# A two-block transformer forward pass: key rotation in its own buffers by two queues, query tiles taken at once, attention steps in pairs

## The chip, the cores and the metric

The kernel runs on one core of one Trainium2 chip. The metric is the device time of one execution in microseconds (us), as the median of several runs. Engines: TensorE (PE, with its weight loads shown as PEld), VectorE (DVE), ScalarE (ACT), GpSimd (POOL) and SyncE (SP), which issues most transfers.

## What is computed

Two layers of different kind run one after the other on a sequence of 512 tokens of width 1024, all in float32. The first has four mixing branches (short convolution, stick-breaking attention, state-space mixer, block attention), a gated merge and a feed-forward part of width 2816. The second, where most of the change lies, is

```python
h = rmsnorm_2(x, norm_g[l])
proj = h @ w_in[l]
q, k, v, za, u, vs, zs, gm = jnp.split(proj, IN_SPLITS_2, axis=-1)
q = partial_rope(q.reshape(B, S, ATT_HEADS, HEAD_DIM), pos)     # 16 heads of 64
k = partial_rope(k.reshape(B, S, ATT_KV_HEADS, HEAD_DIM), pos)  # 2 heads, rotation on 16 of 64 rows
a = window_sink_attention(q, k, v, att_sinks[l])                # 64 queries see 192 keys at most
a = (a * jax.nn.silu(za)) @ w_att_out[l]
sgo = chunked_spatial_gating(gelu(u), gelu(vs), ...)
sgo = (sgo * jax.nn.silu(zs)) @ w_sg_out[l]
ga, gs = jnp.split(jax.nn.sigmoid(gm + b_merge[l]), 2, axis=-1)
x = x + (ga * a + gs * sgo) @ w_o[l]
```

## The kernel before, in words

**Weights in units.** All large products run over units of 256 weight columns (1 MB, eight tiles of 128 rows). SP loads a unit into one of two slots of `raw`; ScalarE rounds it to `whi` (line 1106, `split`); GpSimd subtracts to get the low part `wlo` (line 503, in halves of 128 columns, counted by the semaphore `lo_done`). TensorE then makes each output tile of 128 x 512 from 24 products: for eight rows of weights high by high and high by low (lines 569, 570), and after them eight low by high (line 577). Two units (n = 8 and 11) and the four `vs` units are token-major (`gemm_tm`, lines 591 to 593, 256 columns a product, the three kinds in turn). SP may load unit n once unit n-2 has its low part.

**Banks.** Tile T goes to one of four PSUM banks G[T % 4] and waits (`free_before`) until VectorE has taken tile T-4 (`tile_free`). In the stretch of the second layer's attention only two of them serve products, since the joined pair `gemm23` holds the scores of every odd step (`mix01` those of every even one): from the tiles of unit n_qz+2 on, tile T waits for tile T-2.

**Second layer, first part.** Unit n_e0 holds keys and values of both key heads; then come four pairs p of a query unit (n_qz+2p, two tiles) and a gate unit `za` (n_qz+2p+1, two tiles), then four units `vs` (n_vs to n_vs+3), then n_ga. Every 128 rows of queries hold two heads, and the rotation needs rows 0 to 7 and 8 to 15 of each head exchanged: VectorE writes the product times sine to `rope_s` (line 1988) and times cosine to `rope_q` (1989), SP exchanges rows from `rope_s` into `rope_t` with four transfers (`swap_rotary`, line 454, after both tiles are taken), and VectorE adds (line 1982). In the order of VectorE this sum stands before the first `za` tile of the same pair is taken (line 1511, reached from 1993). The keys use the same `rope_s` and `rope_t`, by eight transfers (line 466), and are summed at line 1905 after the first query product is ready.

**Attention in steps.** 32 steps (8 pairs of heads by 4 blocks of 128 queries) lie between the products. A step s is: scores on TensorE (`w_scores`, line 930, array in quarters of 64 x 64), maximum on VectorE (1919, 1920), exponential on ScalarE (1339, 1341), normalising on VectorE into `wp` (1926, 1927, 1932), transposing on TensorE (`w_turn`, 941), copying on ScalarE (1350, 1352), product with the values on TensorE (`w_values`, 953), and after every fourth step the result times the gate (1940, 1359, 1946). Each engine has a function `w_slot` with a counter `pos`, called at fixed places: on TensorE in each slot i the scores of step i, the values of step i-4, the transposition of step i-3. Slots lie after half of a tile's first part and after every even tile, at most six for each pair p from p = 1, then four in each `vs` unit and four in n_ga.

**The start.** TensorE runs seven idle products on a zero tile (line 645) until the first part of x, the identity and the parameters are in, transposes x tile by tile (`turn_in`, 637) and works on the first weight tile between the transpositions (661 to 663). The identity and the parameters come by ScalarE's queue, x and the weights by SP's.

Of the kernel before, what the change touches and what calls it, by code (L numbers as in the profile page):

```python
# [75 lines left out]
def build_program(nc, x, par, cst1, cst2a, w_in, w_branch, w_o, w_gu, w_down, w_in2, sg_w, sg_b, ln_g,  # L76
# [8 lines left out]
    with ctx:  # L85
# [99 lines left out]
        rope_s = place("rope_s", [P, 2, SEQ], Z0 + 40)  # L185
        za_e = place("za_e", [P, 2, SEQ], Z0 + 12)
# [77 lines left out]
        STEPS, W_PER = KD * TT, 6  # L264

        def w_bank(s):

            return (mix01, gemm23)[s % 2][:, :].rearrange("p (h c) -> p h c", h=2)[:, :, 0:192]

        def w_cols(s, i):  # L270

            return (mix01, gemm23)[s % 2][:, 448 + 4 * i:448 + 4 * i + 2]
# [76 lines left out]
        def _(sp):  # L349
# [12 lines left out]
            a_cols = (IN_XA, IN_BG, IN_CG, IN_X, IN_BC, IN_Z, IN_QD, IN_KD, IN_VD, IN_QB, IN_KB, IN_VB)  # L362
            load_x(0)
# [92 lines left out]
            for p in range(4):  # L456
                for j, c0 in enumerate((I2_Q, I2_ZA)):
# [90 lines left out]
        def _(pe):  # L548
            mm = nc.tensor.matmul

            def gemm_fm(T, n, s, xh, xl, kts, col, first, whi_=whi, wlo_=wlo, hook=None, ready=None):
# [11 lines left out]
                half = (3 * kts // 2 + 1) // 2  # L563
                for k in range(kts):
# [6 lines left out]
                    if hook and k == half - 1:  # L571
                        hook()
# [3 lines left out]
                for k in range(kts):  # L576
                    last = mm(bank[:, :], wlo_[:, s, k, col:col + P], xh[:, k, :], start=False, stop=(k == kts - 1))  # L577
                last.then_inc(sem("tile_done"), 1)

            def gemm_tm(T, n, c0, w_cols, per_bank, hook=None):  # L580
# [4 lines left out]
                pe.wait_ge(sem("lo_done"), 2 * n + 2)  # L585
                for i in range(per_bank):
                    t = i if per_bank == TT else (T % 2) * per_bank + i
                    o = bank[:, i * w_cols:(i + 1) * w_cols]
                    for k in range(KD):
# [9 lines left out]
            def unit_fm(n, xh=hh, xl=hl, kts=KD, after=None, hook=None, ready=None):  # L599
                for j in range(2):  # L600
                    gemm_fm(tiles_before(n) + j, n, n % 2, xh, xl, kts, j * P, j == 0, hook=hook,
# [38 lines left out]
            def first_tile():  # L640

                bank = G[0]
                pe.wait_ge(sem("warm"), 1)
# [54 lines left out]
            def st_cb(g):  # L698
                pe.wait_ge(sem("silu"), 4)
                if g == 0:  # L700
                    pe.wait_ge(sem("dtv_read"), 1)
# [161 lines left out]
            for f, (n0, part, h0) in enumerate(ffn_units):  # L863
                if f == 0:
# [3 lines left out]
                    unit_last_k(n0, hh, hl, KD, ("h2_lo", 0), sum_rows)  # L868
# [16 lines left out]
            unit_last_k(n_e0, hh, hl, KD, ("h3_lo", 0), sum_both, 1)  # L885
# [72 lines left out]
            def w_slot(limit):  # L958
                i = pos[0]
                if i >= limit and limit < STEPS:  # L960
                    return
                if i < STEPS:
                    w_scores(i)
                if 0 <= i - 4 < STEPS:
                    w_values(i - 4)
                if 0 <= i - 3 < STEPS:
                    w_turn(i - 3)
                pos[0] += 1

            for p in range(4):  # L970
                n = n_qz + 2 * p
                lim = W_PER * p
                for u in range(2):
                    for j in range(2):
                        gemm_fm(tiles_before(n + u) + j, n + u, (n + u) % 2, hh, hl, KD, j * P, j == 0,
                                hook=lambda: w_slot(lim))
                        if p == 0 and u == 0:
                            (turn_rows, turn_keys)[j]()
                        if j == 0:
                            w_slot(lim)  # L980
            for p in range(4):
                n = n_vs + p
                for j in range(2):
                    gemm_tm(tiles_before(n) + j, n, 0, UC, 2, hook=lambda: w_slot(STEPS))
# [10 lines left out]
            unit_fm(n_ga, hook=lambda: w_slot(STEPS), after=lambda j: w_slot(STEPS))  # L995
# [95 lines left out]
        def _(act):  # L1091
# [34 lines left out]
            act.dma_start(ident, cst1[:, 0:P]).then_inc(sem("start_in"), 16)  # L1126
            act.dma_start(prm[:, :], par).then_inc(sem("start_in"), 16)
            act.preload_act_table_set(EXP_LN)
            act.wait_ge(sem("start_in"), 32)
# [1035 lines left out]
```

## Time and profile before

| | us |
|---|---|
| Runs | 1363.51, 1366.31, 1366.41; median 1366.31 |
| Profiled execution | 1365.36 |
| its span, first to last instruction | 1363.3 |
| granted TensorE clock, mean over the span | 0.998 |
| TensorE busy | 1347.7 |
| VectorE busy | 615.5 |
| GpSimd busy | 596.7 |
| ScalarE busy | 513.6 |

The ends of matmuls are modelled: one of 128 x 512 is shown with 0.39 us, while the next one starts 0.23 us after it. So the distances between starts tell more of TensorE than its busy time.

### The profile page before, as it was taken

What the parts mean: (1) busy time and instruction counts of PE and PEld (TensorE: products, weight loads), DVE (VectorE), ACT (ScalarE), POOL (GpSimd) and SP (SyncE); (2) the same over time, 40 slices, a digit from 0 to 9 for tenths busy, and PEclk for the clock granted to TensorE, in tenths of its full rate; (3) what the DMA queues carried; (4) which work ended last, traced back from release to release, by engine and by line L of the source; (5) the groups of instructions that cost most, each with busy time, mean ns of one, the idle gap of its engine ahead of it and who ended that gap; (6) DMA issues with size and microseconds to landing.
All of it is one profiled execution on the core that took longest, in us unless ns stands there. A gap on an engine that the chain in (4) does not pass through costs nothing.

```text
span 1363.3 us, 17812 instructions
## 1 busy us (share of the span) xinstructions
PE 1347.7 (99%) x6852; PEld 1107.1 (81%) x6852; DVE 615.5 (45%) x1049; ACT 513.6 (38%) x751; POOL 596.7 (44%) x448
## 2 busy tenths in 40 slices
PE   8999999999999999999999999999999999999998
PEld 7878877788888888888888887777888888888887
DVE  3675434466544533213322347576765332242233
ACT  6222444555532443112221236244554323433233
POOL 4462333334444455444444546433322643525441
PEclk9999999999999999999999999999999999999999
DMA  6231241413223433233323223322221222222221
GB/s 203 80 107 62 78 135 51 147 39 95 72 97 101 147 93 92 93 101 102 105 93 93 85 70 108 101 66 70 94 63 62 94 91 93 93 93 94 92 93 62
DMA packets 146177, 126.43 MB, mean 93 GB/s; under 512 B 4352, under 2 KB 143744, under 8 KB 146112
## 3 DMA queue, kind: packets, MB, share of 16 engines
q1 hardware_dynamic: 145824, 125.40, 29.4%
q8 instruction: 46, 0.75, 0.2%
q10 hardware_dynamic: 288, 0.12, 0.0%
q14 instruction: 19, 0.16, 0.0%
HBM read 120.66 MB, written 2.10 MB: 90 GB/s over the span
## 4 chain that ended last, share of the span: by engine, by line
issue 41%; POOL 29%; PE 28%; ACT 1%; DVE 1%; DMA 0%; POOLq 0%; ACTq 0%; DVEq 0%
POOL wlo L503 28%; PE gemm L569 6%; PE gemm L570 6%; PE gemm L577 6%; PE gemm L591 1%; PE gemm L592 1%; PE gemm L593 1%; POOL wlo_b L499 1%; PE mix L953 1%; PE mix L941 1%; PE mix L1010 1%; PE gemm L619 0%; PE gemm L623 0%; PE gemm L620 0%; DVE sml L2022 0%
## 5 line engine op out<-in xcount | busy, mean ns | idle before, releaser
L503 POOL TENSOR_TENSOR wlo<-raw,whi 128x512 fp32r<-128x512 f32 x424 | 571.4, 1379 | 575.7 <-ACT whi L1106 575.7
L569 PE MATMUL gemm<-hh,whi 128*128 128x512 f32 x1128 | 445.9, 395 | 3.1 <-DVE za L1511 2.7
L570 PE MATMUL gemm<-hl,whi 128*128 128x512 f32 x1128 | 440.3, 390 | 0.0
L577 PE MATMUL gemm<-hh,wlo 128*128 128x512 f32 x1128 | 278.7, 389 | 0.0
L1106 ACT ACTIVATE whi<-raw 128x2048 fp32r<-128x2048 f32 x106 | 202.4, 1910 | 197.6 <-PE gemm L577 166.4
L569 PEld LDWEIGHTS gemm<-hh,whi 128*128 128x128 f32 x1128 | 212.4, 188 | 52.2 <-issue 4.7
L577 PEld LDWEIGHTS gemm<-hh,wlo 128*128 128x128 f32 x1128 | 211.8, 188 | 44.3
L570 PEld LDWEIGHTS gemm<-hl,whi 128*128 128x128 f32 x1128 | 212.5, 188 | 42.9 <-issue 0.2
L499 POOL TENSOR_TENSOR wlo_b<-raw_b,whi_b 128x512 fp32r<-128x512 f32 x16 | 20.7, 1291 | 152.2 <-ACT whi L1106 152.2
L1832 DVE TENSOR_TENSOR fu_t<-gemm,R 128x512 f32<-128x512 f32 x22 | 15.2, 692 | 99.7 <-PE gemm L577 99.7
L591 PE MATMUL gemm<-whi,hh 128*128 128x256 f32 x192 | 56.2, 293 | 0.4 <-POOL wlo L503 0.4
L592 PE MATMUL gemm<-whi,hl 128*128 128x256 f32 x192 | 54.3, 283 | 0.0
L593 PE MATMUL gemm<-wlo,hh 128*128 128x256 f32 x192 | 54.3, 283 | 0.0
L569 PE MATMUL gemm<-ah,whi 128*128 128x512 f32 x132 | 51.4, 390 | 0.5 <-DVE xT L1811 0.5
L570 PE MATMUL gemm<-al,whi 128*128 128x512 f32 x132 | 51.4, 389 | 0.0
L1123 ACT ACTIVATE gt<-gt 128x512 f32<-128x512 f32 x32 | 20.2, 631 | 75.2 <-DVE gt L1779 75.2
L1779 DVE TENSOR_TENSOR gt<-gemm,R 128x512 f32<-128x512 f32 x32 | 22.1, 689 | 57.7 <-PE gemm L577 57.2
L1302 ACT ACTIVATE fg_t<-fg_t 128x512 f32<-128x512 f32 x22 | 13.9, 632 | 84.6 <-DVE fg_t L1830 84.6
L1851 DVE TENSOR_TENSOR xT<-xT,gemm 128x512 f32 x16 | 11.0, 688 | 70.0 <-PE gemm L577 57.0
L591 PEld LDWEIGHTS gemm<-whi,hh 128*128 128x128 f32 x192 | 36.7, 191 | 1.3 <-issue 1.2
L592 PEld LDWEIGHTS gemm<-whi,hl 128*128 128x128 f32 x192 | 36.8, 191 | 0.2 <-issue 0.2
L1830 DVE TENSOR_TENSOR fg_t<-gemm,R 128x512 f32<-128x512 f32 x22 | 15.2, 692 | 48.1 <-PE gemm L577 39.8
(462 smaller groups left out, 1998.4 us busy)
## 6 DMA issues: line engine op xcount, KB each, us to landing
raw<-w_in SPq DMA_DIRECT2D x55, 1024.0 KB, 5.1
raw<-w_gu SPq DMA_DIRECT2D x44, 512.0 KB, 4.7
raw<-w_o SPq DMA_DIRECT2D x8, 1024.0 KB, 4.9
raw<-w_down SPq DMA_DIRECT2D x16, 512.0 KB, 4.0
raw_b<-w_branch SPq DMA_DIRECT2D x16, 256.0 KB, 5.3
raw<-w_ao SPq DMA_DIRECT2D x4, 1024.0 KB, 4.8
raw<-w_so SPq DMA_DIRECT2D x4, 1024.0 KB, 4.9
raw<-w_down SPq DMA_DIRECT2D x8, 384.0 KB, 3.7
```

What stands on the lines that cost most here:

```text
L499: nc.gpsimd.tensor_tensor(a(wlo_b), a(raw_b), as_f32(a(whi_b)), ALU.subtract)
L503: last = nc.gpsimd.tensor_tensor(a(wlo), a(raw), as_f32(a(whi)), ALU.subtract)
L569: mm(bank[:, :], w, xh[:, k, :], start=(k == 0), stop=False)
L570: mm(bank[:, :], w, xl[:, k, :], start=False, stop=False)
L577: last = mm(bank[:, :], wlo_[:, s, k, col:col + P], xh[:, k, :], start=False, stop=(k == kts - 1))
L591: mm(o, hh[:, k, tok], whi[:, s, k, w], start=(k == 0), stop=False)
L592: mm(o, hl[:, k, tok], whi[:, s, k, w], start=False, stop=False)
L593: last = mm(o, hh[:, k, tok], wlo[:, s, k, w], start=False, stop=(k == KD - 1))
L1106: fn(a(whi), a(raw), ACT.Copy).then_inc(sem("hi_done"), 1)
L1123: return fn(dst, src, ACT.Tanh, scale=scale)
L1779: tt(g, G[T % 4][:, :], R[:, :], ALU.mult).then_inc(sem("tile_free"), 1)
L1830: tt(fg_t[:, s, :], G[T % 4][:, :], R[:, :], ALU.mult).then_inc(sem("tile_free"), 1)
```

## The change

- The key rotation gets buffers of its own, `key_s` and `key_t`. Four of its transfers are issued by SP, four by ScalarE, as soon as `key_s` is written; queries no longer wait for the keys' `rope_t`.
- The joined pair of banks is now `gemm01`; products of the attention stretch use banks 2 and 3. Tiles of unit n_qz+2 wait for tile T-4, the restriction to T-2 holds from n_qz+3 to n_ga.
- VectorE takes query tiles directly after their products (`take_q`); in pair 0 the mixing weights, the keys and the constants come between, and the sum of the query pair (`finish_q`) after `za` tile 0 is taken. In the later pairs the order is written out, with slots between.
- An even slot has the scores of steps i and i+1, the values of i-4 and i-3 and the transposition of i-2, an odd slot the transposition of i-2 alone. Slots lie at fixed numbers of products in a tile (`W_AT`).
- Token-major units take all high products of a block first and wait for the low part of the weights after them.
- At the start the identity comes first on SP's queue, nine idle products run before it and eleven after the first two transpositions.
- Semaphores `dtv_read`, `h2_hi`, `h3_hi`, `h2_lo`, `h3_lo` are merged into others that count on.

```diff
@@ buffers and banks
+        key_s = place("key_s", [P, SEQ], Z0 + 80)
+        key_t = place("key_t", [P, 2, SEQ], Z0 + 28)
...
-        G = [ctx.enter_context(nc.psum_tensor(f"gemm{i}", [P, 512], f32)) for i in range(2)]
-        gemm23 = ctx.enter_context(nc.psum_tensor("gemm23", [P, 1024], f32))
-        G = G + [gemm23[:, 0:512], gemm23[:, 512:1024]]
+        gemm01 = ctx.enter_context(nc.psum_tensor("gemm01", [P, 1024], f32))
+        G = [gemm01[:, 0:512], gemm01[:, 512:1024]] + [ctx.enter_context(nc.psum_tensor(f"gemm{i}", [P, 512], f32)) for i in (2, 3)]
...
+        W_AT = ((12,), (4, 20), (12,), (4, 20))
+        W_END = STEPS + 5
...
-            return G[T % 2] if tiles_before(n_qz + 2) <= T < tiles_before(n_ga + 1) else G[T % 4]
+            return G[2 + T % 2] if tiles_before(n_qz + 2) <= T < tiles_before(n_ga + 1) else G[T % 4]
...
-            return T - 1 if tiles_before(n_qz + 2) <= T < tiles_before(n_ga + 2) else T - 3
+            return T - 1 if tiles_before(n_qz + 3) <= T < tiles_before(n_ga + 1) else T - 3
@@ sync
+            sp.dma_start(ident, cst1[:, 0:P]).then_inc(sem("ident_in"), 16)
             load_x(0)
...
                     if p == 0 and j == 1:
-                        sp.wait_ge(sem("tile_free"), tiles_before(n_e0) + 1)
-                        for r in (0, 64):
-                            for a, b in ((0, 8), (8, 0)):
-                                for kv in range(2):
-                                    sp.dma_start(rope_t[r + a:r + a + 8, kv, :], rope_s[64 * kv + b:64 * kv + b + 8, 0, :])\
-                                        .then_inc(sem("rope_in"), 16)
+                        sp.wait_ge(sem("key_s"), 1)
+                        for a, b in ((0, 8), (8, 0)):
+                            for kv in range(2):
+                                sp.dma_start(key_t[a:a + 8, kv, :], key_s[64 * kv + b:64 * kv + b + 8, :]).then_inc(sem("key_in"), 16)
                     if p >= 1 and j == 0:
-                        sp.wait_ge(sem("k_ready"), 1)
                         swap_rotary(p - 1)
@@ tensor, gemm_tm
-                pe.wait_ge(sem("lo_done"), 2 * n + 2)
                 for i in range(per_bank):
...
                     for k in range(KD):
-                        w, tok = slice(c0, c0 + w_cols), slice(t * P, (t + 1) * P)
                         mm(o, hh[:, k, tok], whi[:, s, k, w], start=(k == 0), stop=False)
                         mm(o, hl[:, k, tok], whi[:, s, k, w], start=False, stop=False)
+                    pe.wait_ge(sem("lo_done"), 2 * n + 2)
+                    for k in range(KD):
                         last = mm(o, hh[:, k, tok], wlo[:, s, k, w], start=False, stop=(k == KD - 1))
@@ tensor, first_tile
-                for i in range(7):
-                    mm(M[3][:, 0:P], warm, warm, start=True, stop=True)
-                pe.wait_ge(sem("start_in"), 32)
+                idle_products(9)
+                pe.wait_ge(sem("ident_in"), 16)
                 for m in range(2):
                     turn_in(m)
+                idle_products(11)
@@ tensor, w_slot
-                if i < STEPS:
-                    w_scores(i)
-                if 0 <= i - 4 < STEPS:
-                    w_values(i - 4)
-                if 0 <= i - 3 < STEPS:
-                    w_turn(i - 3)
+                if i % 2 == 0:
+                    for s in (i, i + 1):
+                        if s < STEPS:
+                            w_scores(s)
+                    for s in (i - 4, i - 3):
+                        if 0 <= s < STEPS:
+                            w_values(s)
+                if 0 <= i - 2 < STEPS:
+                    w_turn(i - 2)
@@ scalar
+            act.wait_ge(sem("key_s"), 1)
+            for a, b in ((0, 8), (8, 0)):
+                for kv in range(2):
+                    act.dma_start(key_t[64 + a:72 + a, kv, :], key_s[64 * kv + b:64 * kv + b + 8, :]).then_inc(sem("key_in"), 16)
@@ vector
+            v.memset(key_t[:, :, :], 0.0)
...
+                if i % 2 == 0:
+                    for s in (i, i + 1):
+                        if s < STEPS:
+                            w_soft(s)
+                if between:
+                    between()
+                if i % 2 == 0:
+                    for s in (i, i + 1):
+                        if s < STEPS:
+                            w_norm(s)
...
+                if p == 0:
+                    take_q(0)
+                    mixing_weights()
+                    take_q(1)
+                    finish_keys()
+                    attention_consts()
+                    take_za(0)
+                    finish_q()
+                    scale_x(0)
+                    take_za(1)
+                    scale_x(1)
+                    continue
+                w_slot()
+                take_q(0)
+                w_slot()
+                w_slot(lambda: take_q(1))
+                gate_attention(p - 1)
+                finish_q()
+                w_slot()
+                take_za(0)
+                w_slot(lambda: scale_x(0))
+                w_slot()
+                take_za(1)
+                scale_x(1)
```

## Rows read from the trace of the kernel before

**Rows 1.** Page, part 1: busy time, share of the span and instructions of each engine.
```profile
PE 1347.7 (99%) x6852; PEld 1107.1 (81%) x6852; DVE 615.5 (45%) x1049; ACT 513.6 (38%) x751; POOL 596.7 (44%) x448
```
**Rows 2.** TensorE's waits: line waited at and for, us in total, times, longest.
```profile
PE gemm L569 <- DVE za L1511: 2.7, 1, 2.7
...
PE gemm L591 <- POOL wlo L503: 0.4, 1, 0.4
```
**Rows 3.** Timeline, first query pair: start us, us, engine, line, operation, [idle before].
```profile
855.16 5.50 SPq L466 DMA_DIRECT2D rope_t<-rope_s  x8
...
866.85 2.64 SPq L454 DMA_DIRECT2D rope_t<-rope_s  x4
...
868.98 1.98 PE L577 MATMUL gemm<-hh,wlo 128*128 128x512 f32 x8
...
871.17 1.68 DVE L1982 TENSOR_TENSOR q<-rope_q,rope_t 128x1024 f32<-128x1024 f32 x1 [4.40 <-DMA rope_t<-rope_s]
...
873.63 0.80 PE L569 MATMUL gemm<-hh,whi 128*128 128x512 f32 x1 [2.68 <-DVE za L1511]
...
876.76 0.39 PE L570 MATMUL gemm<-hl,whi 128*128 128x512 f32 x1
```
**Rows 4.** Windows: stretch, us, busy of PE, PEld, DVE, ACT, POOL, clock, DMA, GB/s.
```profile
873.60:877.00 3.40, 3.37 (x9) 2.70 (x10) 2.27 (x3) 0.63 (x1) 0.38 (x1) 0.54 0.62 192
```
**Rows 5.** Timeline, one attention step between products of a query unit.
```profile
920.71 0.39 PE L569 MATMUL gemm<-hh,whi 128*128 128x512 f32 x1
920.94 0.39 PE L570 MATMUL gemm<-hl,whi 128*128 128x512 f32 x1
...
921.25 0.21 PEld L930 LDWEIGHTS gemm<-k,q 64*64 64x64 f32 x8 [0.35 <-issue]
...
921.74 0.42 PEld L953 LDWEIGHTS mix<-wpt,v 128*64 128x64 f32 x8 [0.28 <-issue]
...
921.95 0.57 DVE L1919 TENSOR_REDUCE gemm<-gemm 128x2 f32<-128x384 f32 x1 [0.81 <-PE gemm L930]
922.34 0.42 PEld L941 LDWEIGHTS mix<-c,wp 128*128 128x128 f32 x4 [0.17 <-issue]
...
922.75 0.47 PE L569 MATMUL gemm<-hh,whi 128*128 128x512 f32 x1
923.06 0.39 PE L570 MATMUL gemm<-hl,whi 128*128 128x512 f32 x1
```
**Rows 6.** Timeline, four transpositions between two tiles.
```profile
859.44 0.60 PE L904 MATMUL mix<-c,wpt 128*128 128x128 f32 x4
...
859.79 0.48 PE L569 MATMUL gemm<-hh,whi 128*128 128x512 f32 x1
```
**Rows 7.** Timeline, the start.
```profile
1.06 3.35 PE L645 MATMUL mix<-warm 128*128 128x128 f32 x14 [1.06 <-DVE warm L1524]
...
5.64 1.97 PE L637 MATMUL gemm<-c,xtm 128*128 128x128 f32 x8 [1.22 <-DMA prm<-par]
...
8.94 1.97 PE L637 MATMUL gemm<-c,xtm 128*128 128x128 f32 x8 [1.34 <-DMA xtm<-x]
...
19.59 0.39 PE L569 MATMUL gemm<-hh,whi 128*128 128x512 f32 x1
...
30.47 1.05 PE L830 MATMUL mix<-xbuf,c 128*128 128x128 f32 x8
```
**Rows 8.** Timelines of the vs units: TensorE's slots, one step's softmax.
```profile
973.45 0.56 PE L930 MATMUL gemm<-k,q 64*64 64x192 f32 x8
...
977.77 0.45 PE L930 MATMUL mix<-k,q 64*64 64x64 f32 x8
...
1009.93 0.16 DVE L1926 TENSOR_TENSOR mix<-mix,sml 128x2 f32<-128x2 f32 x1
1010.33 1.12 DVE L1932 TENSOR_TENSOR wp<-mix,sml 64x384 f32<-64x384 f32 x2
...
1010.52 0.41 ACT L1339 ACTIVATE gemm<-gemm,sml 128x192 f32<-128x192 f32 x1
```

More of the change, by code:

```diff
@@ L570, in gemm_fm @@
                     mm(bank[:, :], w, xl[:, k, :], start=False, stop=False)
-                    if hook and k == half - 1:
-                        hook()
+                    if hooks and 2 * k + 2 in hooks:
+                        hooks[2 * k + 2]()
                 if whi_ is whi:
@@ L577, in gemm_fm @@
                     last = mm(bank[:, :], wlo_[:, s, k, col:col + P], xh[:, k, :], start=False, stop=(k == kts - 1))
+                    if hooks and 2 * kts + k + 1 in hooks:
+                        hooks[2 * kts + k + 1]()
                 last.then_inc(sem("tile_done"), 1)
@@ L642, in first_tile, with idle_products @@
                 bank = G[0]
+                def idle_products(count):
+                    for i in range(count):
+                        mm(M[3][:, 0:P], warm, warm, start=True, stop=True)
                 pe.wait_ge(sem("warm"), 1)
-                for i in range(7):
-                    mm(M[3][:, 0:P], warm, warm, start=True, stop=True)
-                pe.wait_ge(sem("start_in"), 32)
+                idle_products(9)
+                pe.wait_ge(sem("ident_in"), 16)
                 for m in range(2):
                     turn_in(m)
+                idle_products(11)
                 for k in range(KD):
@@ L993, in pairs_after_first @@
                             gemm_fm((4 * p + T, T % 4), 2 * p + n0 + u, (n0 + u) % 2, h, l, KD, j * P, j == 0)
-            unit_fm(n_ga, hook=lambda: w_slot(STEPS), after=lambda j: w_slot(STEPS))
+            unit_fm(n_ga, hooks={4: w_slot})
             unit_last_k(n_ga + 1, ath, atl, KD, ("at_lo", 0))
@@ L1353, in w_turned, with w_out, w_slot @@
                 last.then_inc(sem("w_pt"), 1)
[L1355 to L1370 removed]
+            def w_out(m):
+                act.wait_ge(sem("w_o"), m + 1)
+                fn(ath[:, m, :], att_t[:, :], ACT.Copy).then_inc(sem("at_hi"), 1)
+            def w_slot():
+                i = pos[0]
+                if i % 2 == 0:
+                    for s in (i, i + 1):
+                        if s < STEPS:
+                            w_exp(s)
+                if 0 <= i - 2 < STEPS:
+                    w_turned(i - 2)
+                if i % TT == 3 and i >= 7:
+                    w_out((i - 7) // TT)
                 pos[0] += 1
@@ L1584, in st_dtT @@
                     last = tt(dtv[:, a], M[0][:, a], pcol("dtb", 0, 4), ALU.add)
-                last.then_inc(sem("dtv_read"), 1)
-                dve.wait_ge(sem("dtv_read"), 1)
+                last.then_inc(sem("dt_f"), 1)
+                dve.wait_ge(sem("dt_f"), 2)
                 link(ts(dts, dtv, -1.0, None, ALU.mult))
@@ L1878, in _ @@
             link(last)
-            stt(out=rope_s[:, 0, :], in0=G[T % 4][:, :], scalar=DH ** -0.5, in1=cs2[:, 1, :], op0=ALU.mult, op1=ALU.mult)
+            stt(out=key_s[:, :], in0=G[T % 4][:, :], scalar=DH ** -0.5, in1=cs2[:, 1, :], op0=ALU.mult, op1=ALU.mult)\
+                .then_inc(sem("key_s"), 1)
             for kv in range(2):
@@ new lines, in take_q, with finish_q @@
+                def take_q(j):
+                    T = tiles_before(n) + j
+                    tile_ready(T)
+                    tt(rope_s[:, j, :], bank_of(T)[:, :], cs2[:, 1, :], ALU.mult)
+                    tt(rope_q[:, j, :], bank_of(T)[:, :], cs2[:, 0, :], ALU.mult).then_inc(sem("tile_free"), 1)
+                def finish_q():
+                    dve.wait_ge(sem("rope_in"), 64 * (p + 1))
+                    b = 2 * p % 4
+                    tt(q2[:, b:b + 2, :], rope_q[:, :, :], rope_t[:, :, :], ALU.add).then_inc(sem("q_ready"), 1)
+                    dve.wait_ge(sem("q_ready"), p + 1)
@@ new lines, in take_za, with scale_x @@
+                def take_za(j):
+                    m, T = 2 * p + j, tiles_before(n + 1) + j
+                    tile_ready(T)
+                    if 4 <= m < 6:
+                        dve.wait_ge(sem("w_o"), m - 3)
+                    scaled(T, za_tile(m), 0.5)
+                def scale_x(j):
+                    m = 2 * p + j
+                    stt(out=xT[:, m, :], in0=xT[:, m, :], scalar=pcol("fg", m), in1=r1[:, :], op0=ALU.mult, op1=ALU.mult)\
+                        .then_inc(sem("x_scaled"), 1)
@@ L2013, in _ @@
                         gate_attention(3)
[L2014 to L2015 removed]
+                    w_slot()
+            while pos[0] < W_END:
+                w_slot()
             def layer_norm_stats():
```

165 lines of the change are left out of this document (55 added, 110 removed).

## The prediction

> **What bounds the kernel now.** I read the engines' totals first, then TensorE's waits, then the timeline around the longest wait, then the timeline of one attention step. TensorE is busy 99% of the span and the next engine 45% [rows 1], so only three things can shorten the run: time in which TensorE stands still, time at its low clock, and spacing between its instructions that the modelled ends hide. Of standing still the wait view has one large piece, 2.7 us until VectorE has taken a `za` tile, and one of 0.4 us for a low part of weights [rows 2].
>
> The timeline shows that piece [rows 3]. TensorE issues the last eight products of a tile from 868.98, and with 0.227 us from start to start (920.71 to 920.94 in [rows 5]) it would go on at 870.79. It goes on at 873.63: 2.84 us lost. The bank that tile n_qz+2 is to fill is freed only when VectorE takes `za` tile 0, and VectorE stands for 4.40 us before that at the sum that finishes the first query pair (line 1982), which waits for the four swap transfers issued from 866.85. The clock falls after this stop: the granted clock is 0.54 over 873.6 to 877 [rows 4], that is mostly its 1.2 GHz level, and the seven starts from 873.63 to 876.76 [rows 3] take 3.13 us where seven at 0.227 take 1.59: another 1.54 us. The place costs 4.4 us in all.
>
> The hidden spacing is in the 32 attention steps. One step [rows 5]: from the last product at 920.94 to the loads of the scores 0.31 us (0.23 between products); the scores' eight loads take 0.21, then 0.28 us of nothing before the values' loads; after those, 0.17 before the transposes; these go from 922.34 to 922.75; and the first product after them is followed by the next only after 0.31 us.
>
> **The change, part by part.**
> (a) *Query tiles taken at once, tile n_qz+2 in its own banks.* The swap of pair 0 is now finished after `za` tile 0 is taken, and tile n_qz+2 goes to banks 2 and 3, which wait for tiles four back instead of two. VectorE's new row in pair 0: query tile 0 at about 856, the mixing weights' copies (1.8 us), query tile 1 once TensorE has it near 859.5, keys and values to about 863, constants 1 us, `za` tile 0 at 865.5. The swaps go out from about 861, so have landed by 866 (2.6 us of issue and 1.7 until line 1982 starts, as in [rows 3]), and tile n_qz+2 asks only for query tile 1. The wait goes with its clock loss: minus 4.4. What is late next is pair 0's finished query, near 868, wanted by the first scores near 873.7: 6 us of slack.
> (b) *Key swaps by two queues.* Eight transfers now take SP 5.5 us [rows 3] and hold back the next weight load until 860.7 (855.16 and 5.50). Afterwards SP has four and ACT four, and they start when the keys' product is written (about 852.4) instead of at 855.2. SP's next load goes about 5 us earlier, which nothing needs at once: zero. ACT's four (0.7 us each by SP's row, 2.8 in all) and the wait stand in front of its split of unit n_qz+1, which then begins near 855 (852.4 and 2.8); it ends near 857, GpSimd's first half near 859.5, and TensorE asks for them at 859.8 and 863.3. Cover 2.8 us, cost zero; without it each us late is a us of stop. The two added memsets of VectorE (0.9 us) lie where it waits for ScalarE: zero.
> (c) *Steps in pairs.* A slot with an even number has two scores, two values, one transposition; an odd slot one transposition alone. Per pair one entry goes (0.31 less 0.23: 0.09) and one turn from scores to values and one from values to transposes, of which only the part that is not streaming is won: of the 0.28 us some 0.12 (192 columns in two passes are 0.16 at 2.4 GHz), of the 0.17 some 0.06. The lone transposition costs 0.35 (859.44 to 859.79, [rows 6]) instead of 0.41. Together 0.33 us. The end of the chain has one slot fewer. I take 0.34 for each of 16 pairs: minus 5.5. Bounds: 0 if the drains are all work, and 0.09 + 0.28 + 0.17 = 0.54, so 8.6 us, if none is.
> The Trainium skill ("TensorE: Matmul & The Clock Gate", section "Architectural detail: the array is 16× 32×32, not 1× 128×128") says that weight loads are pulled ahead of matmuls in flight; were that so between these forms, pairing would win nothing and the sum would be 5.5 us smaller. "TensorEngine Tiling (Array Packing)", section "Key Properties", of the same skill has it that a change of tiling mode drains the engine; the rows go with this one, since the loads do stand off.
> (d) *Order of the products in the token-major units.* Low parts of the weights are asked for after 16 products instead of before the first. The 0.4 us wait [rows 2] goes, with the restart about it: minus 0.6. In number and form the products are the same.
> (e) *The start.* The identity goes first on SP, 20 idle products instead of 7. Seven take 3.35 us from 1.06; the first transposes start at 5.64, the second at 8.94 when more of x has landed, and the first tile is over at 19.59 [rows 7]. With nine the engine works until 5.4, then on the first transposes, then on eleven more. At the low clock eleven take 11 × 0.48 = 5.3 us, from 7.5 to 12.8; at the high clock 11 × 0.26 = 2.9 (four products in 1.05, [rows 7]), from about 6.6 to 9.5. If they bring the high clock before the second transposes, those and the next eight products run at half their time, which the landing of x and the chain through ScalarE partly take back. I take minus 1.0. Bounds: plus 2, if the eleven run at the low clock and push everything, minus 2.5, if all that is slow between 8.94 and 13 is won.
> (f) Merged semaphores, the moved mixing weights and constants, the bank split itself: they move no work of TensorE. Zero; their cover is VectorE's free time.
>
> Sum: 4.4 + 5.5 + 0.6 + 1.0 = 11.5. The profiled execution took 1365.4 us (span 1363.3); the median of the runs, 1366.3, is 0.07% above it and inside the runs' own scatter. 1365.4 - 11.5 = 1353.9.
>
> **Rivals.**
> *Pairing wins nothing* (the drains are streaming). For it: the ends are modelled. Against it: entry and exit gaps are seen in starts. 1365.4 - 6.0 = 1359.4.
> *The stop comes back elsewhere in the first pair*: ScalarE's split behind key swaps, or tile n_qz+3, which now is the first to wait for a tile two back. Against it: slack of 2.8 us and more. Its price is the old one, 4.4: 1358.3.
> *The idle products cost*: 3 us against my term: 1356.9.
> *Slower: the next pair waits for the softmax of the last.* Before, a step's softmax had another step's time to spare; now the scores of a pair need both weights of the previous pair. Slots lie 4.32 us apart in the vs units (973.45 to 977.77, [rows 8]), so a pair has 8.3. Chain: scores to first reduction 0.7 us (921.25 to 921.95, [rows 5]), two of these 1.4, ScalarE 1.25 per step from 1010.52, then VectorE from line 1926 to the end of line 1932 1.5 per step (1009.93 to 1011.45): about 6.0. The slack is 2.3, and about as much where a query tile is taken between. It decides where the chain grows by 2.3 + 0.9: at 0.9 us per pair the 11.5 and a further 2.7 are gone. At 1.5 us per pair: 1353.9 + 24 = 1378.
>
> **How the numbers follow.** About 0.2% (2.7 us) is what a measurement of this kernel can tell from no change. Forecast 0.68; pairing wins nothing 0.11; stop elsewhere 0.09; idle products 0.05; softmax waits 0.07, of which 0.03 so mild that the sum lands within 0.2%. Faster 0.93, same 0.03, slower 0.04. I predict 1354.0. Range: down to 1349.5 (pairs at their upper bound, 3 us more, and 1.5 of scatter), up to 1361 (the first rival and 1.5).
>
> **What would show it.** The wait for line 1511 gone, the granted clock 1.0 from 871 to 884; the L591 wait gone; in an even slot two scores with one gap of loads behind, and in an odd slot transposes alone; from the first query unit to the end of the attention about 10 us less; the second transposes near 9 with high-clock spacing. It would be wrong if TensorE had waits at line 930 or 941 for VectorE's `wp`, or if an even slot took as long as two old ones.

## The result, and the profile after

The changed kernel takes 1353.92 us (median of four runs, 1353.55 to 1354.07) against 1366.05 us of the kernel before on the same chip (four runs, 1363.51 to 1366.41). The ratio is 0.9911, with an interval of 0.9899 to 0.9924. The forecast was 1354.0. The profiled execution took 1353.55 us, 11.8 less than the one before. The total is right; of its terms the start and the pairing are too small, one loss was missing, and these errors nearly cancel, as the rest shows.

Part 1 of the changed kernel's page, to be laid beside [rows 1]:

```profile
PE 1341.1 (99%) x6878; PEld 1110.9 (82%) x6878; DVE 619.2 (46%) x1050; ACT 513.2 (38%) x751; POOL 597.9 (44%) x448
```

TensorE remains the bound. Its 26 further instructions are thirteen more idle products at the start, two each, and yet it is busy for fewer us. Its waits, beside [rows 2] (line waited at and for, us in total, times, longest):

```profile
PE mix L649 <- DVE warm L1533: 1.1, 1, 1.1
PE gemm L623 <- issue: 0.9, 1, 0.9
...
PE gemm L570 <- ACT whi L1113: 0.4, 1, 0.4
...
PE mix L961 <- DVE att_t L1952: 0.4, 1, 0.4
```

The 2.7 us at a `za` tile and the 0.4 us for a low part are gone, and so are the two waits for x and the parameters at the start. One is new: the values' product waits 0.4 us for the gated output `att_t`. Waits of 0.2 us and less at transposes fall below the list.

Where the clock was at half speed [rows 4], it is now full for the whole first query pair. But another stretch has it at half, at 101.8 us. The windows of the changed kernel (columns as in [rows 4]):

```profile
98.40:101.80 3.40, 3.40 (x27) 3.18 (x26) 1.17 (x3) 0.00 (x0) 1.47 (x2) 1.00 0.23 42
101.80:105.20 3.40, 3.40 (x9) 2.62 (x9) 0.73 (x2) 0.00 (x0) 0.00 (x0) 0.50 0.76 267
...
870.00:884.00 14.00, 14.00 (x88) 10.79 (x87) 8.56 (x22) 5.92 (x21) 5.28 (x5) 1.00 0.24 76
```

The same stretch in the kernel before:

```profile
101.80:105.20 3.40, 3.40 (x22) 3.04 (x22) 1.21 (x4) 0.00 (x0) 0.37 (x1) 1.00 0.56 175
```

TensorE is busy throughout in both. With the granted clock at 0.50, its 1.2 GHz level, the products start 0.43 us apart instead of 0.23. The timeline of TensorE in the changed kernel shows what stands before the fall:

```profile
98.93 2.29 PE L702 MATMUL mix<-sml,c 128*128 128x4 f32 x20
101.08 0.49 PE L570 MATMUL gemm<-hh,whi 128*128 128x512 f32 x1
101.40 0.40 PE L571 MATMUL gemm<-hl,whi 128*128 128x512 f32 x1
...
101.93 0.63 PE L571 MATMUL gemm<-hl,whi 128*128 128x512 f32 x1
102.36 0.63 PE L570 MATMUL gemm<-hh,whi 128*128 128x512 f32 x1
102.78 0.63 PE L571 MATMUL gemm<-hl,whi 128*128 128x512 f32 x1
```

Twenty products of only four columns, the state mixer's cumulative sums, take 2.15 us from the first one's start to the next wide product; 0.7 us after that the clock falls. Laid beside the kernel before, product by product, the lead shrinks over these 3.4 us from 1.99 to 0.43: the fall costs 1.55 us. Nothing in the diff touches that place.

The start, beside [rows 7]:

```profile
1.06 4.21 PE L649 MATMUL mix<-warm 128*128 128x128 f32 x18 [1.06 <-DVE warm L1533]
5.06 1.60 PE L641 MATMUL gemm<-c,xtm 128*128 128x128 f32 x8
6.50 2.62 PE L649 MATMUL mix<-warm 128*128 128x128 f32 x22
8.96 1.04 PE L641 MATMUL gemm<-c,xtm 128*128 128x128 f32 x8
...
17.60 0.39 PE L570 MATMUL gemm<-hh,whi 128*128 128x512 f32 x1
```

The second transposes start at the old moment but at the high clock (1.04 us for eight instructions instead of 1.97), and the first tile is over at 17.60 instead of 19.59: 2.0 us gained. The clock's record in this trace begins with its rise to full speed at 6.21 us, during the first transposes and before the eleven idle products begin at 6.50.

Two slots of the attention, beside [rows 5, 6], an even one and then an odd one:

```profile
920.00 0.39 PE L571 MATMUL gemm<-hl,whi 128*128 128x512 f32 x1
920.32 0.21 PEld L938 LDWEIGHTS mix<-k,q 64*64 64x64 f32 x8 [0.35 <-issue]
...
921.13 0.90 PEld L961 LDWEIGHTS mix<-wpt,v 128*64 128x64 f32 x16 [0.28 <-issue]
...
922.20 0.20 PEld L949 LDWEIGHTS mix<-c,wp 128*128 128x128 f32 x2 [0.17 <-issue]
...
922.40 0.48 PE L570 MATMUL gemm<-hh,whi 128*128 128x512 f32 x1
...
922.72 0.39 PE L571 MATMUL gemm<-hl,whi 128*128 128x512 f32 x1
```

```profile
906.01 0.39 PE L571 MATMUL gemm<-hl,whi 128*128 128x512 f32 x1
906.25 0.60 PE L949 MATMUL mix<-c,wp 128*128 128x128 f32 x4
...
906.91 0.39 PE L571 MATMUL gemm<-hl,whi 128*128 128x512 f32 x1
```

The gaps of 0.28 and 0.17 us are of the same size as before, but come once for two steps. A slot costs what it lengthens the distance between products by: 922.72 - 920.00 less two paces of 0.227 is 2.27 us for the even one, 906.91 - 906.01 less the same is 0.45 for the odd one. The old step in [rows 5] costs 1.67. Summed from such starts, all slots together take 49.77 us before (36 slots) and 43.77 now (34): 6.0 less. Four steps in the middle of the stretch take 6.13 before and 5.29 now, which is 0.42 per pair.

**Where the 11.8 us are.** The sums of squares that precede the second layer's units start at 844.90 instead of 845.35: 0.45 gained so far, 2.0 at the start less 1.55 by the clock. From there to the last product of the branch's output projection it is 202.42 us (to 1047.32) instead of 213.75 (to 1059.10): 11.33, of which 4.4 are the stop, 6.0 the slots, 0.6 the wait for a low part, and 0.3 I did not trace. The rest of the kernel took the same time.

### The profile page after: what moved, and what is told of

Read it like the earlier page. It is cut to its first block, busy times and chain, and to the rows that moved or that the text cites. A ratio compares the mean times of both kernels' runs of the same rounds, so it can differ in the third digit from the quotient of the medians.

```text
span 1351.5 us, 17866 instructions
## 1 busy us (share of the span) xinstructions
PE 1341.1 (99%) x6878; PEld 1110.9 (82%) x6878; DVE 619.2 (46%) x1050; ACT 513.2 (38%) x751; POOL 597.9 (44%) x448
## 4 chain that ended last, share of the span: by engine, by line
PE 96%; DVE 2%; ACT 1%; issue 0%; DMA 0%; SPq 0%; ACTq 0%; DVEq 0%
PE gemm L570 25%; PE gemm L571 25%; PE gemm L578 25%; PE gemm L623 2%; PE gemm L624 2%; PE gemm L627 2%; PE gemm L593 2%; PE gemm L597 2%; PE gemm L594 2%; PE mix L961 1%; PE mix L949 1%; PE mix L1017 1%; PE mix L776 1%; PE mix L649 0%; PE mix L800 0%; PE mix L759 0%
## 5 line engine op out<-in xcount | busy, mean ns | idle before, releaser
L593 PE MATMUL gemm<-whi,hh 128*128 128x256 f32 x192 | 48.8, 293 | 0.0
L594 PE MATMUL gemm<-whi,hl 128*128 128x256 f32 x192 | 47.0, 282 | 0.0
L1849 DVE TENSOR_TENSOR al<-fu_t,ah 128x512 f32 x22 | 34.7, 1576 | 2.7
```

The lines of the kernel that those rows point to most:

```text
L1849: tt(flat(al), fu_t[:, s, :], as_f32(flat(ah)), ALU.subtract).then_inc(sem("act_lo"), 1)
```

## The experiments

The kernel before ran beside each on the same chip, at 1366.2 to 1366.4 us.

### Only the banks, and only the order

The forecast gave 4.4 us to two edits together. Each was put into the kernel before by itself. The banks:

```diff
-  return G[T % 2] if tiles_before(n_qz + 2) <= T < tiles_before(n_ga + 1) else G[T % 4]
+  return G[2 + T % 2] if tiles_before(n_qz + 2) <= T < tiles_before(n_ga + 1) else G[T % 4]
...
-  return T - 1 if tiles_before(n_qz + 2) <= T < tiles_before(n_ga + 2) else T - 3
+  return T - 1 if tiles_before(n_qz + 3) <= T < tiles_before(n_ga + 1) else T - 3
```

> The kernel before with the bank change alone (joined pair of banks 0 and 1, products of the attention stretch in banks 2 and 3, the wait for the tile two back from unit n_qz+3 on); VectorE keeps its old order. My theory: the stop of 2.84 us in the first query pair goes, because the first tile of unit n_qz+2 no longer needs za tile 0, and with it the low-clock stretch (1.5 us): 4.4 us less, about 1361.5 us. Rival (the stop comes back at the next tile that needs a tile two back): a new wait on TensorE before unit n_qz+3 or at the first scores, and less than 2 us gained.

And VectorE's order in pair 0:

```diff
-  if u == 1 and j == 0:
-      dve.wait_ge(sem("rope_in"), 128 + 64 * (p + 1))
-      b = 2 * p % 4
-      tt(q2[:, b:b + 2, :], rope_q[:, :, :], rope_t[:, :, :], ALU.add).then_inc(sem("q_ready"), 1)
-      dve.wait_ge(sem("q_ready"), p + 1)
+  if u == 1 and j == 0 and p:
+      finish_q()
   tile_ready(T)
...
   scaled(T, za_tile(m), 0.5)
+  if j == 0 and p == 0:
+      finish_q()
```

> The kernel before with the order alone changed: in the first query pair VectorE takes za tile 0 before it waits for the swapped rows; banks as before. My theory: za tile 0 is taken near 866, tile n_qz+2 finds its bank free at 870.8 and the same 4.4 us go: about 1361.5 us. Rival (both the banks and the order are needed): the wait stays, or moves to the second tile of unit n_qz+2, which then waits for za tile 1 behind the late sum, and little is gained.

Measured: 1360.65 us (0.996, 0.9948 to 0.9972) and 1361.12 us (0.9964, 0.995 to 0.9978). In both the wait for `za` is gone and the windows of the two kernels, first the banks and then the order, show the full clock:

```profile
870.00:884.00 14.00, 14.00 (x78) 10.25 (x78) 11.22 (x23) 6.55 (x21) 8.13 (x7) 1.00 0.51 151
```

```profile
870.00:884.00 14.00, 14.00 (x79) 10.25 (x78) 10.69 (x22) 5.92 (x20) 8.13 (x7) 1.00 0.49 153
```

From the last of the sums of squares to the first scores it is 28.25 us in both, against 32.66 before: 4.41, the forecast's 4.4. So the price was right, and either edit alone earns all of it; the change holds both, and the second earns nothing. The medians fell by more, 5.8 and 5.3 us beside the kernel before, whose own runs there spread from 1363.2 to 1367.7. The profiled executions fell by 4.9 and 4.5, of which 0.5 in the kernel with the banks was gained at the start, where the edit changes nothing. It is the traces that give the 4.4.

### Only the start, and parts of it

Into the kernel before:

```diff
+  sp.dma_start(ident, cst1[:, 0:P]).then_inc(sem("ident_in"), 16)
   load_x(0)
...
-  for i in range(7):
-      mm(M[3][:, 0:P], warm, warm, start=True, stop=True)
-  pe.wait_ge(sem("start_in"), 32)
+  idle_products(9)
+  pe.wait_ge(sem("ident_in"), 16)
   for m in range(2):
       turn_in(m)
+  idle_products(11)
```

ScalarE's queue keeps the parameters alone.

> The kernel before with the change of the start alone (identity first on SP, 9 and 11 idle products). Theory from the two traces: the first tile is over 2.0 us earlier (17.6 instead of 19.6 us) and the wait of 4.4 us in the query pair stays. If the clock falls during the cumulative sums near 100 us here too, 0.45 us are left of it (about 1365.5 us); if that fall was chance, 2.0 us are gained. Rival: the idle products do nothing for the start by themselves, and the 2.0 us came from chance of the clock: first tile over near 19.6.

The same with seven idle products and none of the eleven:

```diff
-  idle_products(9)
+  idle_products(7)
...
-  idle_products(11)
```

> The kernel before with the identity first on SP's queue and the parameters alone on ScalarE's, but still seven idle products and none after the first transpositions. Theory: the identity's place gives what the first transpositions start earlier (5.0 instead of 5.6 us), but the clock stays low to about 10 to 13 us, so that the first tile ends at 19 to 19.6. Rival: the identity's place is all of the gain and the first tile ends near 17.6.

And the changed kernel with its nine, without the eleven:

```diff
-  idle_products(11)
```

> The changed kernel without the eleven idle products after the first transpositions. Theory: nine idle products and the transpositions already bring the high clock near 6.2 us; without the eleven TensorE stands for 2.3 us until the next part of x is there, and the clock holds or falls by chance; the first tile ends between 17.6 and 19.6. If the eleven are needed, it ends later than 18.5 and the kernel is 1 to 2 us slower than the changed one; if they are not, the same within 0.5 us.

Measured: 1364.72 us (0.9992, 0.9982 to 1.0001), 1365.87 us (0.9994, 0.9984 to 1.0004) and 1352.89 us (0.9906, 0.9889 to 0.9922). In their traces the first tile is over at 17.51, 19.08 and 18.61 us. TensorE's timeline without the eleven, and its windows:

```profile
5.00 1.04 PE L641 MATMUL gemm<-c,xtm 128*128 128x128 f32 x8
8.30 1.97 PE L641 MATMUL gemm<-c,xtm 128*128 128x128 f32 x8 [2.27 <-DMA xtm<-x]
```

```profile
5.00:8.00 3.00, 1.03 (x10) 0.79 (x8) 1.46 (x3) 2.21 (x3) 0.01 (x1) 1.00 1.08 340
8.00:12.00 4.00, 3.70 (x15) 3.22 (x16) 2.64 (x4) 1.38 (x2) 2.50 (x2) 0.57 1.14 329
...
101.80:105.20 3.40, 3.40 (x18) 2.83 (x19) 1.20 (x3) 0.00 (x0) 0.00 (x0) 1.00 0.93 284
```

Without the eleven, TensorE stands 2.27 us for x, the clock falls again after that, and the first tile is over 1.0 us later than with them. So the eleven are worth 1.0 at the start by these two traces; other traces with the same start end the first tile between 17.15 and 18.03. They do not bring the high clock, they keep it: without them the first transposes take 1.04 us, the pace of the full clock, and the second 1.97. In the kernel before, the identity's place alone gives 0.5 (19.08 for 19.59) and all of the start 2.1 (17.51). Still the kernel without the eleven is faster than the changed one, by 0.6 us of the profiled executions and 1.0 of the medians: its clock does not fall at 101.8. In these two traces the later fall more than takes back what the eleven earn. The eleven alone do not bring that fall about: the kernel before with the same start does not show it. Of the two timings in the kernel before neither can be told from no change, by its interval; the traces show what lies beneath.

### Single steps in the changed kernel

```diff
-  if i % 2 == 0:
-      for s in (i, i + 1):
-          if s < STEPS:
-              w_scores(s)
-      for s in (i - 4, i - 3):
-          if 0 <= s < STEPS:
-              w_values(s)
-  if 0 <= i - 2 < STEPS:
-      w_turn(i - 2)
+  if i < STEPS:
+      w_scores(i)
+  if 0 <= i - 4 < STEPS:
+      w_values(i - 4)
+  if 0 <= i - 3 < STEPS:
+      w_turn(i - 3)
...
-  unit_fm(n_ga, hooks={4: w_slot})
+  unit_fm(n_ga, hooks={4: w_slot, 20: w_slot})
```

ScalarE's and VectorE's slots follow, and the sum of the query pair stands one slot later.

> The changed kernel with the attention steps one by one again, at the new places (36 slots; one score, one value product, one transposition each); all else as changed, but the sum of a query pair one slot later. My theory: pairing is worth what the slots of the two traces differ in, 6.0 us: about 1360 us, and each slot on TensorE as long as in the kernel before (1.49 us for a full step). Rival (pairing wins nothing, the gain came from the order of VectorE and the even spacing of slots): within 1 us of the changed kernel.

Measured: 1358.84 us (0.995, 0.9933 to 0.9966), span 1355.8. The 36 slots take 49.77 us again, exactly the old sum. The clock does not fall at 101.8:

```profile
101.80:105.20 3.40, 3.40 (x17) 2.79 (x16) 0.31 (x1) 0.00 (x0) 0.00 (x0) 1.00 0.65 230
```

Its first tile is over at 17.16, 0.44 before the changed kernel's. The spans differ by 4.3, and that is the 6.0 of the slots and 0.3 that I did not trace, less 1.55 for the fall and 0.44 for the start. The spans alone would have priced pairing 1.7 us too low.

### Keys' transfers on one queue

```diff
   for kv in range(2):
-      sp.dma_start(key_t[a:a + 8, kv, :], key_s[64 * kv + b:64 * kv + b + 8, :]).then_inc(sem("key_in"), 16)
+      for r in (0, 64):
+          sp.dma_start(key_t[r + a:r + a + 8, kv, :], key_s[64 * kv + b:64 * kv + b + 8, :]).then_inc(sem("key_in"), 16)
...
-  act.wait_ge(sem("key_s"), 1)
-  for a, b in ((0, 8), (8, 0)):
-      for kv in range(2):
-          act.dma_start(key_t[64 + a:72 + a, kv, :], key_s[64 * kv + b:64 * kv + b + 8, :]).then_inc(sem("key_in"), 16)
```

> The changed kernel with all eight key transfers on SP, none on ScalarE. My theory: the second queue is worth nothing here, since the keys' sum waits for the second query tile (near 860) and not for the transfers (issued from about 852 to 857.5): same time as the changed kernel within 0.5 us, no new wait on TensorE. Rival: SP's next load of weights comes 3 us later and the sum of the first query pair with it, and TensorE waits at the first scores: 1 us or more slower.

Measured: 1353.45 us (0.991, 0.9894 to 0.9927), span 1351.5, the changed kernel's to the tenth. The queues' rows, two of the changed kernel and then those with one queue:

```profile
852.00 2.82 SPq L470 DMA_DIRECT2D key_t<-key_s  x4
852.00 3.70 ACTq L1341 DMA_DIRECT2D key_t<-key_s  x4
...
854.87 0.45 SPq L359 DMA_DIRECT2D raw<-w_in  x1
```

```profile
851.95 5.49 SPq L471 DMA_DIRECT2D key_t<-key_s  x8
857.49 0.44 SPq L359 DMA_DIRECT2D raw<-w_in  x1
```

SP's next weight load goes 2.6 us later, and nothing waits for it. The second queue is worth nothing here. The Trainium skill ("DMA: Bandwidth & Descriptors", section "Issuing engines are not separate DMA queues") says that starting transfers from several engines saves only the time to issue them; the trace agrees, with 5.49 us of issue on one queue against 2.82 beside 3.70.

### How much slack the softmax has

Six chained reductions of 128 x 512 stand on VectorE in each even slot, ahead of the normalising. Their result is not used.

```diff
   if i % 2 == 0:
+      for _ in range(6):
+          link(v.reduce_max(sml[:, 252:253], R[:, :], AX.X))
       for s in (i, i + 1):
```

> The changed kernel with six reductions over 512 columns more on VectorE in every even slot, between the maxima and the normalising (about 3.9 us), their result unused. It measures the slack of the pair's softmax. My forecast put the slack at 2.3 us: then TensorE waits 1.6 us at the scores of most of 15 pairs, 20 to 25 us slower than the changed kernel, with waits for wp in the trace. If the slack is 4 us or more, under 5 us are lost; if the slack was nearly used up, over 40 us are lost.

Measured: 1395.21 us (two runs, 1395.16 and 1395.26; 1.0216, 1.0196 to 1.0236), 41.7 us of span above the changed kernel, where 20 to 25 were expected. A row of VectorE and TensorE's waits:

```profile
1009.62 4.28 DVE L1969 TENSOR_REDUCE sml<-R 128x1 f32<-128x512 f32 x6
```

```profile
PE mix L961 <- DVE att_t L1952: 10.3, 6, 3.0
PE mix L949 <- ACT wpt L1361: 8.2, 5, 3.9
PE gemm L938 <- DVE wp L1946: 6.0, 8, 1.1
PE mix L949 <- ACT wpt L1363: 3.1, 1, 3.1
```

The slots total 78.56 us, 34.8 more, or 2.2 per pair. The six took 4.28 us, so on the mean some 2.1 of a pair were absorbed. That is near the 2.3 which the forecast took for the slack, but it is a mean over unlike pairs: some lose nothing, one loses 6.4 us, and slots that fall into a stretch of low clock count as longer too. In the changed kernel itself the slack of one pair among the `vs` units can be read directly:

```profile
994.60 0.56 PE L938 MATMUL mix<-k,q 64*64 64x192 f32 x8
...
999.34 1.12 DVE L1946 TENSOR_TENSOR wp<-gemm,sml 64x384 f32<-64x384 f32 x2
...
1003.03 0.34 PE L938 MATMUL mix<-k,q 64*64 64x64 f32 x6
```

The chain from the scores to the last weights is 5.9 us long, and 2.6 are left until the next pair's scores. The other 6.9 of the 41.7 lie outside the slots. In this run the clock falls six further times during or just after the attention, behind such waits, as here:

```profile
1008.00:1011.40 3.40, 1.06 (x9) 0.86 (x8) 3.23 (x8) 2.33 (x12) 1.38 (x1) 1.00 0.19 33
1011.40:1014.80 3.40, 2.80 (x16) 2.83 (x17) 3.19 (x7) 1.05 (x4) 0.00 (x0) 0.66 0.79 275
```

The largest waits are not at the scores, which the slower rival named, but at the values' product and the transposes, which want the gated output and the copies to have emptied their banks.

### The fall at 101.8, and the small waits

Two theories had come up: that the run of twenty narrow products lets the clock fall, and that the sum of the query pair, put ahead of the softmax in VectorE's order, makes the small waits in the slots. The changed kernel was run again beside three variants. First the narrow products in two parts: twelve within a tile and eight where all twenty were.

```diff
-  def st_acs():
+  def st_acs(ns=(3,)):
...
-      for n in range(TT):
+      for n in ns:
...
-  unit_fm(n, after=after)
+  unit_fm(n, after=after, hooks={12: lambda: st_acs((0, 1, 2))} if n == 7 else None)
```

Then, in the later pairs, the sum behind a gate tile and behind the maxima of a slot:

```diff
   gate_attention(p - 1)
-  finish_q()
   w_slot()
   take_za(0)
-  w_slot(lambda: scale_x(0))
+  w_slot(finish_q)
   w_slot()
+  scale_x(0)
   take_za(1)
```

The third variant has both edits. The changed kernel again, the parted products, the later sum, and both:

> The changed kernel as it is, beside the next three on the same chip: 1353 to 1354 us. If the fall of the clock near 101.8 us in its trace was chance, a new trace can be without it and then 1.5 us shorter; if it belongs to the kernel, it is there again.

> The changed kernel with the cumulative sums of the state-space mixer (20 products of 4 columns in one run of 2.15 us) split: 12 of them in the middle of the tile before, 8 at its end. Theory: the clock fell there because TensorE had 2.15 us of almost empty products in one run; with full products between, it stays high, and 1.5 us less the 0.2 us of one more change of form are gained where the changed kernel shows the fall: about 1.3 us faster than the changed kernel. Rival: the fall has another cause (it comes a fixed time after the first rise): the clock falls near 102 us all the same, and the time stays.

> The changed kernel with VectorE's sum of a query pair (from p = 1 on) moved behind the maxima of the next even slot, in the place of the scaling of x, which moves behind it. Theory: the small waits of the query stretch that the changed kernel still has (0.44 us for att_t and values, 0.25, 0.19 and 0.12 us at lone transpositions, 1.0 us in all) come from that sum standing before maxima and gates on VectorE; they go, and 0.8 to 1.0 us are gained. Rival: they belong to ScalarE's order (the copy of the transposed weights behind two exponentials) and stay.

> The two last edits together: if they are independent, their gains add up, to about 2.2 us below the changed kernel, 1351.5 us; no new wait.

| | median us | ratio, interval | profiled span | second transposes at | clock falls near 102 | slots, us |
|---|---|---|---|---|---|---|
| changed, again | 1353.18 | 0.9899, 0.9882 to 0.9915 | 1351.1 | 8.51 | yes | 43.83 |
| products in two parts | 1352.18 | 0.9894, 0.9877 to 0.991 | 1350.4 | 9.38 | no | 43.80 |
| later sum | 1352.33 | 0.9891, 0.9874 to 0.9907 | 1350.8 | 9.37 | yes | 42.72 |
| both | 1350.67 | 0.9884, 0.9867 to 0.99 | 1348.5 | 8.46 | no | 42.72 |

The windows, of the changed kernel again, of the parted products, and of both:

```profile
101.80:105.20 3.40, 3.40 (x11) 2.71 (x10) 0.30 (x1) 0.00 (x0) 0.00 (x0) 0.64 0.67 233
```

```profile
101.80:105.20 3.40, 3.40 (x16) 2.75 (x16) 1.20 (x3) 0.00 (x0) 0.00 (x0) 1.00 0.87 294
```

```profile
101.80:105.20 3.40, 3.40 (x17) 2.79 (x16) 0.39 (x1) 0.00 (x0) 0.00 (x0) 1.00 0.68 237
```

The medians of the four lie 2.5 us apart, and their intervals overlap, so the timings alone do not tell them apart; the spans of the traces do, and they add up. Without the fall 1.55 us go, with the later sum 1.1 (43.83 less 42.72), and where the second transposes start 0.9 later the span is longer by that: 1351.1 - 1.55 + 0.9 is 1350.4, 1351.1 - 1.1 + 0.9 is 1350.9, and 1351.1 - 1.55 - 1.1 is 1348.4. The wait for `att_t` and the delays at lone transposes are gone in both traces with the later sum, and the slots take 43.8 us in all five traces of the pairs that keep the old place and have no added work. So the second theory is shown, for the sum together with the scaling of x, which the edit moves too.

The first is shown only together with a second condition. Of the twelve traces that have the twenty products in one run, the clock falls right behind them in five and not in seven. The kernel before with the new start is one of the seven, though its run begins at nearly the same moment as the changed kernel's:

```profile
98.86 2.29 PE L699 MATMUL mix<-sml,c 128*128 128x4 f32 x20
```

```profile
101.80:105.20 3.40, 3.40 (x16) 2.81 (x15) 0.69 (x1) 0.00 (x0) 0.00 (x0) 1.00 0.79 276
```

What sets the five apart is the time since the clock's first rise, with which its record begins in each trace (in two of them, identity alone and without the eleven, it had fallen and risen once more by 12.2 us):

| traces | the run begins after the rise, us | fall |
|---|---|---|
| later sum; one queue; changed; added reductions; changed again | 92.26; 92.72; 92.72; 93.03; 93.19 | 95.57 after the rise, in all five |
| single steps; start alone; identity alone; without the eleven | 93.71; 93.82; 95.05; 95.04 | none |
| order alone; before; banks alone | 87.69; 87.78; 88.12 | none |

The changed kernel's windows from its rise to its fall, and over the fall:

```profile
6.21:101.78 95.57, 95.34 (x473) 78.40 (x472) 59.45 (x102) 36.15 (x46) 50.27 (x36) 1.00 0.42 127
101.78:105.19 3.41, 3.41 (x10) 2.63 (x9) 0.75 (x2) 0.00 (x0) 0.00 (x0) 0.50 0.77 268
```

So the rival by which the fall comes a fixed time after the first rise has the moment right; whether it comes goes with the place of the run and with its being unbroken. For the latter the parted products and the later sum are a close pair: the clock rises at 7.10 and 7.05 us, the unbroken run is followed by the fall and the parted one is not. All four executions with the parted run have a mean granted clock of 0.999. With both edits an unbroken run would have begun 93.5 us after the rise, by an estimate from the changed kernel again, and so between the two groups; that trace tells less. The grouping was found in the finished traces and no run was made to test it; one that shifts the unbroken run alone by 1 us would.

Among the runs of the changed kernel again one took 1351.48, 1.7 under the median, and of the later sum one 1350.39, 1.9 under; that is about the size of this fall, and their mean granted clock is 0.999 where the others have 0.997 and 0.998. It fits an execution without the fall, but those executions were not profiled.

## Why the prediction was right, and where it was not

**(a) The stop, 4.4: right.** 4.41 measured twice, stop and clock together. What the forecast didn't separate is that each of its two edits is enough.

**(b) Two queues for the keys, 0: right,** shown by one queue giving the same span. ScalarE's four transfers took 3.70 us where 2.8 was reckoned from SP's row, so its split began at 855.81 instead of 855; the cover held.

**(c) Pairing, 5.5: right in kind, 0.5 too small, by two errors.** A pair saves 0.42 instead of 0.34 where nothing waits. The entry gives the 0.09 forecast. The lone transposition costs 0.353 as [rows 6] had it. With 0.06 for it and the 0.09, 0.27 of the 0.42 are left for the drains: of 0.45 us (0.28 and 0.17) I took 0.18 as idle. That makes 6.7 for 16 pairs, and 7.05 with the shorter ends of the chain, as the later sum shows (49.77 less 42.72). Against that, 1.05 us are lost to waits that the forecast did not have: at four places VectorE, with the sum of the query pair in front, is later than its slack allows (0.28, 0.15, 0.4 and 0.2 us). The step that failed here is the one saying of slack "and about as much where a query tile is taken between". The rival by which pairing wins nothing is out: single steps put into the changed kernel bring the 6.0 us of slots back. The Trainium skill ("TensorEngine Tiling (Array Packing)", section "Key Properties") says that changing the tiling mode drains TensorE; the trace agrees, with 0.28 and 0.17 us of nothing before the loads of the next form.

**(d) Low parts of the weights later, 0.6: agrees** with the traces, where the gap of 0.6 over the product pace is gone. It was not run alone.

**(e) The start, 1.0: half its size.** The first tile is over at 17.60 instead of 19.59, so 2.0 us are gained, and in other traces with the same start between 1.6 and 2.4 (18.03 with the parted products, 17.15 when the changed kernel ran again). I had the high clock for the second transposes, and took back more of it for the landing of x than was lost. The way to it was not as I had it: I let the eleven products bring the high clock, but it is there at 6.21, before they begin, and what they do is keep it.

**Missing: the clock at 101.8, minus 1.55.** No term or rival of the forecast had a fall of the clock at a place that the change does not touch; the step that failed is to count the clock only where TensorE stands still. Start and fall together give 0.45, where 1.0 was forecast; pairing gives 0.5 more than forecast, and 0.3 is untraced. By the profiled executions 11.8 us went, where 11.5 were forecast: the total is right partly by luck. Without the fall at 101.8 the same change would have won 13.4.

**The rivals.** The slower one, that the next pair waits for the softmax, had the slack nearly right (2.6 us at the pair read above, 2.1 on the mean, 2.3 forecast) and does not decide. Its slope was too mild: 2.2 per pair cost 41.7 us and not 35, since behind the waits the clock falls too, which my 24 us for 1.5 per pair left out. "The stop comes back elsewhere" and "the idle products cost" didn't happen: no new wait of the old size stands in the traces of the changed kernel or of either single edit, and the eleven products earn 1.0 at the start.

## What to carry to other kernels

Changes of operand form on TensorE are worth counting: batching two steps per slot saved 0.42 us per pair, and the starts of the neighbouring products show it where the modelled ends do not. When two edits of a change serve the same stall, price them once, and try each alone. When experiments differ by a microsecond or two, read the granted clock along the whole span first: an edit at the start can shift what the clock does far away, and 1.55 us of it hid a quarter of the pairing's gain.

## What the runs showed of the hardware

The clock fell while TensorE was shown busy without a gap: after 2.15 us of twenty four-column products, in five of twelve traces, for 3.4 us, with products 0.43 us apart instead of 0.23. In these five the run began 92.3 to 93.2 us after the clock's first rise and the fall came 95.57 us after it; where the run began at 93.7 to 95.1 or at 87.7 to 88.1, there was none. The other falls read here came after TensorE had stood still: 2.84 us at the `za` tile, 2.27 us for x.

After a stop of nearly the same kind the clock stayed low for 3.4 us in the kernel before, but for 6.8 in the kernel with the identity first and no eleven idle products (from 872.4), and that alone is worth over a microsecond between two traces.

Eight transfers of 8 rows took SP 5.49 us to issue, 0.69 each; on ScalarE's queue four took 3.70, 0.93 each.
